# The conditioning vector activated in place: every tensor behind it starts 32 bytes lower

## What is computed

```python
def peer(x, wq, subkeys, u, v):          # first layer, per block of 128 tokens
    ...
    ue = u[eidx]                          # eidx: 128 tokens x 8 heads x 16
    ve = v[eidx]
    act = gelu(einsum('td,thkd->thk', xb, ue))
    return einsum('thk,thkd->td', gates * act, ve)

def ada_modulation(c, ada_w, ada_b):      # second and third layer
    m = jax.nn.silu(c) @ ada_w + ada_b
    return jnp.split(m, N_MOD, axis=-1)
```

## The kernel before

| tensors | past a multiple of 256 |
|---|---|
| `ring`, `hT`, `sq`, `rstd`, `lnv`, `cols` | 128 |
| `ones`, `ident`, `mcol` | 0 |
| `gain` | 128 |
| `silc` (byte 86528, 32 bytes long) | 0 |
| `small` (byte 86560), `xn`, `arena` (byte 95008), and in their place later `xh`, `second`, `fh`, `fl`, `yh`, `yl`, `dhi`, `dlo`, `xl`, `whi`, `wlo`, `sqh` | 32 |

## Time and profile before

### The profile page before, as it was taken

One profiled execution on the slowest core, in us unless ns is written; L12 is line 12 of the kernel. 1 busy time (PEld: TensorE's weight loads), 2 busy tenths in 40 slices (PEclk: granted clock), 3 DMA queues, 4 the chain that ended last, 5 costly groups with the idle time before them and its releaser, 6 DMA issues.

```text
span 1539.4 us, 20597 instructions
## 1 busy us (share of the span) xinstructions
PE 1363.7 (89%) x7648; PEld 1028.7 (67%) x7648; DVE 1025.9 (67%) x1830; ACT 503.1 (33%) x848; POOL 587.4 (38%) x630
## 2 busy tenths in 40 slices
PE   8899897778877777877788799999999999999998
PEld 7788896334422222322233299999999996899998
DVE  5996769958566675768444568678777467554544
ACT  2222212211121211231111165544435577444342
POOL 1420055777776777777777400022220003000000
PEclk9999999899999999999999999999999999999999
DMA  9956597999999999999999866688984441344540
GB/s 376 329 213 209 217 404 279 410 409 409 409 411 409 409 409 409 409 409 409 409 409 410 353 233 213 229 315 319 318 292 158 144 166 48 124 165 172 196 163 27
DMA packets 114078, 454.16 MB, mean 295 GB/s; under 512 B 12048, under 2 KB 29600, under 8 KB 100816
## 3 DMA queue, kind: packets, MB, share of 16 engines
q0 software_dynamic: 81616, 297.84, 49.4%
q1 hardware_dynamic: 32384, 155.31, 27.7%
HBM read 452.06 MB, written 1.05 MB: 294 GB/s over the span
## 4 chain that ended last, share of the span: by engine, by line
PE 50%; DMA 27%; DVE 10%; POOL 6%; issue 5%; ACT 1%; SPq 1%; DVEq 0%; POOLq 0%; ACTq 0%
PE psum L2253 16%; DMA arena<-v_d,arena 14%; DMA arena<-u_d,arena 10%; PE psum L1862 8%; PE psum L2267 8%; POOL arena L540 6%; DVE arena L1396 3%; PE psum L1805 3%; PE psum L2144 3%; PE psum L1893 2%; DMA arena<-w_ada 1%; PE psum L2093 1%; PE psum L1920 1%; DMA arena<-w_peerq 1%; PE psum L2001 1%
## 5 line engine op out<-in xcount | busy, mean ns | idle before, releaser
L2144 PE MATMUL psum<-arena 128*128 128x512 f32 x952 | 470.4, 620 | 139.1 <-DMA arena<-v_d,arena 122.4
L2144 PEld LDWEIGHTS psum<-arena 128*128 128x128 f32 x952 | 164.5, 191 | 405.8 <-DMA arena<-v_d,arena 263.3
L1396 DVE CUSTOM_DVE_ANT_0 arena<-arena,psum 128x1024 f32<-128x1024 f32 x256 | 306.3, 1219 | 187.6 <-DMA arena<-u_d,arena 186.6
L540 POOL DMA_INDIRECT arena<-u_d,arena x256 | 243.1, 950 | 148.5 <-issue 53.4
L540 POOL DMA_INDIRECT arena<-v_d,arena x256 | 241.4, 943 | 80.0 <-issue 68.0
L1064 DVE TENSOR_TENSOR wlo<-ring,whi 128x2048 fp32r<-128x2048 f32 x69 | 158.1, 2292 | 86.4 <-ACT whi L608 86.4
L775 ACT ACTIVATE arena<-ident,arena 128x128 f32<-128x128 f32 x238 | 89.5, 397 | 364.1 <-PE psum L2144 325.3
L2253 PE MATMUL psum<-xh,whi 128*128 128x256 f32 x704 | 202.1, 287 | 1.6 <-DVE xl L1058 1.4
L2253 PE MATMUL psum<-xl,whi 128*128 128x256 f32 x704 | 199.2, 283 | 0.0
L2253 PE MATMUL psum<-xh,wlo 128*128 128x256 f32 x704 | 199.1, 283 | 0.0
L608 ACT ACTIVATE whi<-ring 128x2048 fp32r<-128x2048 f32 x69 | 131.2, 1902 | 23.6 <-PE psum L1862 18.9
(11 more groups left out here) (310 smaller groups left out, 2295.3 us busy)
## 6 DMA issues: line engine op xcount, KB each, us to landing
ring<-w_ffn SPq DMA_DIRECT2D x44, 1536.0 KB, 6.7
second<-w_ada POOLq DMA_DIRECT2D x64, 384.0 KB, 6.0
arena<-w_ada SPq DMA_DIRECT2D x50, 384.0 KB, 7.5
ring<-w_inproj SPq DMA_DIRECT2D x14, 1024.0 KB, 8.0
ring<-w_qkv SPq DMA_DIRECT2D x12, 1024.0 KB, 4.9
ring<-w_l0in SPq DMA_DIRECT2D x10, 1024.0 KB, 5.6
ring<-w_peerq SPq DMA_DIRECT2D x6, 1024.0 KB, 8.5
sq<-w_ada SPq DMA_DIRECT2D x14, 384.0 KB, 7.0
```

Source lines behind the costliest of these rows:

```text
L540: g.indirect_dma_start(S["rows"][:, p % GRING, :], None, u_d if kind == "u" else v_d, bass.IndirectOffsetOnAxis(S["idx"][:, n // SLOTS, n ...
L1396: v.tensor_tensor_reduce(row, row, xrow[n // SLOTS], 1.0, 0.0, ALU.mult, ALU.add, S["act"][:, n // SLOTS, n % SLOTS:n % SLOTS + 1]).then_i ...
L2144: ins = t.matmul(vacc[tt][:, at], S["diag"][:, c % DIAGS, :], row[:, at], start=(n % SLOTS == 0), stop=(n == LAST_PE[tt]))
```

## The change

The tensor `silc` is no longer declared; the name stands for the eight columns "c" of `cols`, and the Silu reads and writes them in place. `cols` itself and all that is declared before `silc` stay where they are. `small` now starts where `silc` did, and it and all tensors behind it lie 32 bytes lower, at multiples of 256 bytes. `ada_ops` reads `silc` as before.

```diff
         gain = sb("gain", [P, 4, 8])
-        silc = sb("silc", [P, 8])
+        silc = cols[:, COL["c"][0]:COL["c"][0] + 8]
         small = sb("small", [P, 64])
...
-            a.activation(silc[:, :], col("c", 0, 8), ACT.Silu).then_inc(silc_ready, 1)
+            a.activation(silc, silc, ACT.Silu).then_inc(silc_ready, 1)
```

## The result

The changed kernel takes 1526.32 us, the median of four runs between 1524.91 and 1527.20, against 1542.07 us for the kernel before: a ratio of 0.9883, with a 95% interval from 0.9863 to 0.9903. It is faster: by 1.2% by that ratio, by 15.75 us or 1.0% by the two medians. The forecast of no change, with its range of 1537.0 to 1547.0 us, is wrong.

What follows compares the result with a forecast made beforehand. The prediction took DMA to bound the gather and PE the split matmuls. Silu, gather, PE and DVE each counted 0, leaving 1539.4 us of span and 1542.0 us of run, range 1537.0 to 1547.0 us, no change at 0.71.

Steps and rivals of the forecast that it cites:

- What bounds the kernel: Whole kernel: gather, some 585 us (300 to 885), bound by DMA into the arena; split matmuls bound by PE.
- The price of a start for the DMA: Gather: 4 KiB packets cost 164 ns at 32 past, 163 ns aligned, so zero gain, bounds 3.6 us either way.
- The second comparison: w_ada's 1536-byte rows: 390 GB/s into `sq` (128 past), 383 and 389 into the arena; starts differ less than stretches.
- The first: Gather: each misaligned row moves 32 bytes too many, 129 units for 128; 4.5 us less, 1537.5 us; chance 0.13.
- The second: Gather: a row costs 17 lines instead of 16, 34 us, capped by POOL's issue at 19 us: 1523 us; chance 0.06.
- its three signs: In the gather: 420 GB/s or more, DMA share under 1.00, and POOL at L540 on the chain.
- the `ident` row: Profile row of `ident` arriving at an aligned start: 12 packets of 4 KiB, 163 ns each, semaphores included.
- The engines: PE and DVE reading moved tensors: zero change, bounds 1.4 us either way for PE, 0.2 us for DVE.
- The slower rival: Split matmuls pay for their new starts, 4.4 us per ns a matmul; 1546.4 us at 1 ns; chance 0.07.
- The Silu in place: In-place Silu before `ada_ops`: costs nothing, with 3.0 us of cover; at most 0.21 us would show without it.

Runs made afterwards that it cites:

- the transfers alone: Kernels with the computation removed, only DMA loads of u_d at chosen starts, executed once each; 4096-byte rows: 420 GB/s at multiples of 256, 408 to 410 otherwise.
- the half rows: Changed kernel with each gather fetching 2048 bytes per partition instead of 4096, half the retrieval work left out; ratio 0.9779 to the kernel before.

## Why the prediction was wrong, point by point

*What bounds the kernel* was read rightly: the gather by DMA, the split matmuls by PE, and what DMA gained, the kernel gained. (The shares given for PE and DVE hold up to 800 us; between 800 and 860 us PE was busy 86% and DVE 47%.) The 585 us that the prediction gave to the gather, times 31 ns in 1281, is an estimate of 14 us, against the 13.4 us measured inside it. The 31 and the 1281 ns are from the means of the page's slices 7 to 21, 409.3 GB/s before and 419.5 after: the gather's 524288 bytes take 1281 ns at the one and 1250 at the other.

*The price of a start for the DMA* is the step that failed: the gather's term of the sum, put at 0 with bounds of 3.6 us, measured 13.4 us. It said that a packet to an aligned start was "not cheaper by more than 1 ns in 164", from 163 ns for `ident` against 164 for the gather. Both numbers charged the time of small packets to the large ones. The page of the kernel before has 12048 packets under 512 bytes; the trace gives each as 4 bytes, and it has as many steps of semaphores by DMA, 16 for each of 753 transfers. So the 4-byte packets are those of the semaphores. The trace lists size and time of each packet. In the stretch of the earlier trace rows it has 1246 of 4 bytes and 9983 of 4096, in that of the earlier trace rows 6 and 12 on POOL's queue (all of `ident`, 64 KB, came in 16 packets of 4096 bytes, each eight of its rows of 512). So the mix is not the same. A small one takes 9 ns in both stretches, a large one 159.0 ns for `ident` and 163.0 on average for the gather. So `ident` was overcharged by 0.5 x 9 = 4.5 ns a packet and the gather by 0.125 x 9 = 1.1, and a difference of 4 ns was read as one of 1. After the change the gather's large packets take 159.2 ns, what `ident` had shown. I also took the rounding of the share as the only error.

*The second comparison*, w_ada into `sq` against the arena, couldn't have told much: each of the three stretches is 1 us long, and the transfers alone show a price only after some 4 us with pieces of 1 KiB and 6 us with 2 KiB. Both starts there, 128 and 32 past, are also wrong starts, and the transfers alone show one rate for all of these, 408 to 410 GB/s with rows of 4096 bytes. A start in a table of starts was treated as a scale (32 is worse than 128, 0 is best), where for the gather's rows it is a yes or no.

*The rivals.* The first, that 32 bytes too many are moved, had the right stretch, the right place and the wrong price: 0.8%, where the transfers alone show 2.7% for a piece of 4096 bytes. It gave 1537.5 us. The second had a whole line as the price, 34 us of the 585, capped by POOL's 1.24 us for a gather at 19 us: 1523 us. That is 3 us from the median measured, 1526.3, and its course is the nearest to the one measured: DMA moves the aligned rows faster (419 to 421 GB/s against 409 to 411), and POOL's L540 is what then appears on the chain (6% to 12%). Of its three signs two came, about 420 GB/s and L540; the DMA share stayed at 1.03. Its price was too high (435 GB/s, where transfers alone reach 420), so that it is its cap that brings it near, and the cap itself came in a little late: POOL's pace over the whole stretch is 1.256 us, not 1.240. It was dismissed with a chance of 0.06, on the strength of the `ident` row. That a line has 256 bytes was supposed in both. No run shows a line; what they show is 420 GB/s at a multiple of 256 and 408 to 410 at the seven other starts, and the 409 of the gather at 32, 64, 96 and 128 past.

*The engines.* The zero held. The split matmuls of the changed kernel, L2253, which the trace had at one start only (start, us, what), to be set beside the earlier trace rows:

```profile
998.57 5.76 PE psum L2253 x48
```

5.76 us for 48, as before. Of the DVE operations the one from `second` is at 1012 ns in both and those from `sq` and from the arena at 1017 or 1018. POOL's L540 has a median of 937 ns before and after. The slower rival falls with the matmuls.

*The Silu in place.* It cost nothing, as forecast; in the changed kernel's profile it ends at 22.97 us and DVE needs it at 24.77 us, a cover of 1.8 us where it was 3.0.

*The range* was built from the rounding of the rows and not from what the rows could not tell apart. With the small packets taken out, 4 ns of 164 would have stood as the gain, and 14 us below 1542.

## What to carry to other kernels

Where a long stretch is bound by DMA into SBUF, look at the start of the target in its partition first: in the transfers alone a multiple of 256 bytes or not is worth 2.7% at pieces of 4 KiB and 32% at 512 bytes, and here a tensor of 32 bytes declared ahead was enough to lose the 2.4% of the gather's rate. Try it on the target that bounds, since `ring` and `sq` at 128 past lost nothing in the changed kernel. When a packet's time is worked out from a queue's share, take out the small packets first or compare equal mixes; here the mixes differed by 2% and hid the gain. And ask what comes next before counting the gain: here POOL's issue stood 2% behind, and the half rows show that a still faster DMA gives nothing more inside the gather.

## What the runs showed of the hardware that I had not expected

In long stretches of transfers alone, rows of 4096 bytes whose target starts 4, 16, 32, 64, 96, 128 or 192 bytes past a multiple of 256 all move at 408 to 410 GB/s, against 420 at a multiple, on POOL's queue and on SP's. At 32 past the price is 4 to 5 ns a piece from 1 to 8 KiB and 7 ns at 512 bytes (384 GB/s aligned, 290 not), and a source 32 bytes into a row costs nothing. Four things stay open: why an engine pays at all; why the price is higher at 512 bytes; why it takes up to some 12 us of such transfers to appear; and why the ring's rows of 8192 bytes and w_ada in `sq`, both 128 past, do not pay in the changed kernel, while the ring's packets take 314 ns in the kernel before and 309 after the change, which did not move them.
